# Feed-forward groups of 3, 6, 6, 7 chunks in place of 4, 6, 6, 6, with two block splits moved into the first seven-product step

## What is computed

```python
def swiglu(h, w_gate, w_up, w_down):
    return (jax.nn.silu(h @ w_gate) * (h @ w_up)) @ w_down

x = x + 0.5 * swiglu(rms_norm(x, norm_g[layer, 0]), ffn_w_gate[layer, 0], ffn_w_up[layer, 0], ffn_w_down[layer, 0])
```

## Time and profile before

| | us |
|---|---|
| median of 3 runs | 1987.91 (1987.78 to 1988.09) |
| profiled execution | 1988.24 |
| its span, first to last instruction | 1986.4 |
| PE busy | 1978.6 (13462 matmuls) |
| DVE busy | 1418.2 |
| ACT busy | 932.5 |
| POOL busy | 964.0 |
| granted clock of TensorE | 0.999 of full speed |

### The profile page before, as it was taken

How to read it: one execution, slowest core, us unless ns; L and a number is a source line. 1 busy time by engine, 2 the same in 40 slices (tenths; PEclk the granted TensorE clock), 3 DMA queues, 4 the chain that set the end, 5 groups by cost and what they waited for, 6 DMA issues and landing times. The chain is left out here.

```text
span 1986.4 us, 35197 instructions
## 1 busy us (share of the span) xinstructions
PE 1978.6 (100%) x13462; PEld 1957.5 (99%) x13462; DVE 1418.2 (71%) x2263; ACT 932.5 (47%) x1642; POOL 964.0 (49%) x1043
## 2 busy tenths in 40 slices
PE   9999999999999999999999999999999999999998
PEld 8999999999999999999999999999999999999998
DVE  5778687664766667878766668778767866878665
ACT  6354454543434435445455345454545535455443
POOL 2556666632000055676663336666743355666643
PEclk9999999999999999999999999999999999999999
DMA  6232324323222223232432222323332223232412
GB/s 162 74 86 70 101 70 117 101 58 95 66 64 65 56 73 86 77 95 69 117 102 75 64 65 75 96 80 91 102 109 70 67 57 86 77 99 65 122 38 86
DMA packets 312853, 165.28 MB, mean 83 GB/s; under 512 B 15539, under 2 KB 310271, under 8 KB 312688
## 3 DMA queue, kind: packets, MB, share of 16 engines
q1 hardware_dynamic: 307840, 157.31, 28.4%
q0 software_dynamic: 2672, 4.65, 1.0%
q10 hardware_dynamic: 2176, 1.07, 0.2%
HBM read 159.01 MB, written 4.00 MB: 82 GB/s over the span
## 5 line engine op out<-in xcount | busy, mean ns | idle before, releaser
L2401 POOL TENSOR_TENSOR sums<-in_raw,sums 128x256 f32<-128x256 f32 (+1 forms) x416 | 440.1, 1088 | 12.1 <-DVE in_lo L1751 3.9
L2401 POOL TENSOR_TENSOR sums<-in_raw 128x256 f32<-128x256 f32 (+1 forms) x208 | 179.9, 885 | 429.7 <-DVE in_lo L1751 377.4
L895 PE MATMUL psum<-xg_hi,in_lo 128*128 128x320 f32 x1152 | 356.0, 309 | 0.0
L893 PE MATMUL psum<-xg_hi,in_hi 128*128 128x320 f32 x1152 | 355.9, 309 | 0.0
L894 PE MATMUL psum<-xg_lo,in_hi 128*128 128x320 f32 x1152 | 355.9, 309 | 0.0
L1751 DVE TENSOR_TENSOR in_lo<-in_raw,in_hi 128x1024 fp32r<-128x1024 f32 (+1 forms) x208 | 271.9, 1309 | 42.5 <-ACT in_hi L1306 42.2
L893 PE MATMUL psum<-mix_hi,in_hi 128*128 128x320 f32 x864 | 267.0, 309 | 0.0
L894 PE MATMUL psum<-mix_lo,in_hi 128*128 128x320 f32 x864 | 267.0, 309 | 0.0
L895 PE MATMUL psum<-mix_hi,in_lo 128*128 128x320 f32 x864 | 267.0, 309 | 0.0
L1306 ACT ACTIVATE in_hi<-in_raw 128x1024 fp32r<-128x1024 f32 (+1 forms) x208 | 205.0, 991 | 111.7 <-PE psum L895 111.7
L744 PE MATMUL psum<-xg_hi,in_hi 128*128 128x320 f32 x800 | 252.3, 315 | 0.9 <-DVE in_lo L1792 0.6
(11 more groups left out here) (267 smaller groups left out, 4560.9 us busy)
## 6 DMA issues: line engine op xcount, KB each, us to landing
in_raw<-in_ffn_w_gate SPq DMA_DIRECT2D x87, 512.0 KB, 5.2
in_raw<-in_ffn_w_up SPq DMA_DIRECT2D x86, 512.0 KB, 4.0
in_raw<-in_ffn_w_down SPq DMA_DIRECT2D x64, 384.0 KB, 4.0
out_raw<-in_ffn_w_down SPq DMA_DIRECT2D x32, 384.0 KB, 3.5
out_raw<-in_ffn_w_down SPq DMA_DIRECT2D x32, 256.0 KB, 2.9
in_raw<-in_mix_w_in SPq DMA_DIRECT2D x14, 512.0 KB, 4.6
out<-y_nat SPq DMA_DIRECT2D x5, 512.0 KB, 3.1
in_raw<-in_mix_w_in SPq DMA_DIRECT2D x8, 256.0 KB, 4.5
```

The lines of the kernel that those rows point to most:

```text
L893: pe.matmul(dst, w_hi[:, k], v_hi, start=k == 0 and slot in (0, 1, 4), stop=False, skip_group_check=True)
L895: end = pe.matmul(dst, w_lo[:, k], v_hi, start=False, stop=k == wide - 1, skip_group_check=True)
L2401: last = pool.tensor_tensor(to[:, part], a[:, part], b[:, part], op)
```

## The change

The groups become 3, 6, 6, 7: one chunk of each feed-forward is no longer classical at the input but has a seven-product step in group 3. The numbers of units and splits are now derived from `PLAIN`; the six input units are listed in `PLAIN_UNITS`. Group 3 gets a seventh hidden slot (`last_hi`, `last_lo`, over the weight sums) and wider tiles for its output weights; its upper half is kept in `pair_even`, and so the sum of squares is cleared only behind the group's last hidden split. The output banks of group 3 move by one, as its last step has the other parity.

The block splits get a new order. T3 is split behind the sixth and now last input unit; B11 and B21 at (0, 1) of the output units; T2 at (1, 1), on DVE behind a wait for T4's source; T1 at (1, 3). B22 and T4 go into the first seven-product step: B22 ahead of its first copy, T4 behind the splits of the second step's first weights. The weights of the first step stay at (2, 3), (3, 1) and (3, 3).

The core of the diff:

```diff
-GROUPS = (4, 6, 6, 6)
+GROUPS = (3, 6, 6, 7)
+PLAIN_UNITS = [(0, 0), (1, 0), (0, 1), (1, 1), (2, 0), (2, 1)]
+LAST_K = GROUPS[3]
...
+        last_hi = over("last_hi", [P, TOKENS], arena + 30720, F32R)
+        last_lo = over("last_lo", [P, TOKENS], arena + 33280, F32R)
+        last_out_hi = over("last_out_hi", [P, 2, LAST_K, P], OUT_HI, F32R)
+        last_out_lo = over("last_out_lo", [P, 2, LAST_K, P], OUT_LO, F32R)
...
+            return 4 + (q + (g == 3)) % out_banks(g, i)
...
-        BLOCKS = ["T3", "T2", "B11", "B21", "T1", "T4", "B22"]
+        BLOCKS = ["T3", "B11", "B21", "T2", "T1", "B22", "T4"]
...
 def before_k(k):
     if g == 0 and i == 0 and j == 0 and k == 0:
-        pe.wait_ge(hidden_lo, 44 * index + 2 * gk - (2 if half == 0 else 0))
+        pe.wait_ge(hidden_lo, 44 * index + 2 * gk - (1 if half == 0 else 0))
...
 # ACT, in_step
+                if s % N_STEPS == 0:
+                    block_split("B22")
                 copy(s, fast, 0)
...
+                if s % N_STEPS == 0:
+                    act.wait_ge(block_made, 8 * index + MADE["T4"])
+                    act.wait_ge(block_lo, 7 * index + BLOCKS.index("T1") + 1)
+                    block_split("T4")
...
 # DVE, in_step
+                if s % N_STEPS == 0:
+                    block_split(index, "B22")
                 if behind:
                     gate_high(s - 1, fast - 1)
...
+                if s % N_STEPS == 0:
+                    block_split(index, "T4")
                 if behind:
                     lower_split(index, g, i - 1)
...
 # DVE, ffn (ACT has the matching lines)
+                    if q == 5:
+                        block_split(index, "T3")
 
                 def blocks_between(i, q):
-                    if (i, q) == (0, 3):
+                    if (i, q) == (0, 1):
                         block_split(index, "B11")
                         block_split(index, "B21")
                     elif (i, q) == (1, 1):
-                        block_split(index, "T1")
+                        dve.wait_ge(block_made, 8 * index + MADE["T4"])
+                        block_split(index, "T2")
                     elif (i, q) == (1, 3):
-                        block_split(index, "T4")
-                    elif (i, q) == (2, 1):
-                        block_split(index, "B22")
+                        block_split(index, "T1")
                     elif (i, q) == (2, 3):
...
+                        dve.wait_ge(hidden_lo, hidden_at(index, g, gk - 1, 1))
+                        for half in range(2):
+                            dve.memset(ss[:, half], 0.0).then_inc(ss_cleared, 1)
```

More of the change, by code:

```diff
@@ L27 @@
 SEVEN = (1, 2)
-assert sum(GROUPS) == FT and max(GROUPS) == SLOTS
+assert sum(GROUPS) == FT and len(PLAIN_UNITS) == 2 * PLAIN
 CHUNK, WINDOW, HD = 64, 128, 64
@@ L137, in weight_slot, with ends @@
     return 7 if slot == 5 and s % N_STEPS % 2 else slot
+def ends(fast):
+    return fast % FAST in (5, 11, 18)
 def read_at(fast, which):
-    order = ("low gate", "high up", "high gate") if fast % 6 == 5 else ("low gate", "high gate", "high up")
+    order = ("low gate", "high up", "high gate") if ends(fast) else ("low gate", "high gate", "high up")
     return 3 * fast + order.index(which) + 1
 def copy_at(fast, slot):
-    return 3 * fast + ((0, 2, 4) if fast % 6 == 5 else (0, 4, 2)).index(slot) + 1
+    return 3 * fast + ((0, 2, 4) if ends(fast) else (0, 4, 2)).index(slot) + 1
 def hidden_at(index, g, i, half):
@@ L876, in out_unit @@
                     before_k(k)
[L877 to L878 removed]
+                    last = product(psum[:, 4 + v % banks if bank is None else bank, 0:HALF], weights[0][:, d % 2, k], weights[1][:, d % 2, k],
+                                   moving[0](k), moving[1](k), k == 0, k == group_k - 1)
                 last.then_inc(out_mm, 1)
@@ new lines, in ffn @@
+                for q, (f, half) in enumerate(PLAIN_UNITS):
+                    b = q % 2
+                    u = 44 * index + q
+                    plain = 2 * PLAIN * index + q
+                    unit = IN_UNIT[phase] + q
+                    bank = in_bank(phase, q)
+                    if q in (0, 2) and index:
+                        norm_factor(m, half)
+                    if q == 2 and not index:
+                        start_factor(1)
+                    dve.wait_ge(in_mm, unit + 1)
+                    wait(dve, hidden_done, u - 1)
+                    dve.tensor_tensor(t1[:, b], psum[:, bank, 0:HALF], rstd[:, half], ALU.mult).then_inc(gate_scaled, 1)
+                    wait(dve, hidden_lo, u - 1)
+                    dve.tensor_tensor(f_t2[b], psum[:, bank + 1, 0:HALF], rstd[:, half], ALU.mult).then_inc(in_read, 1)
+                    if q == 0 and not index:
+                        start_factors(1)
+                    dve.wait_ge(silu_done, plain + 1)
+                    dve.wait_ge(in_read, unit + 1)
+                    dve.tensor_tensor(f_t2[b], f_t2[b], t1[:, b], ALU.mult).then_inc(hidden_done, 1)
+                    hidden_split(f, half, u + 1, f_t2[b])
+                    if index == 0 and q == 3:
+                        out_lo_split(f_out_hi, f_out_lo, 0, 0, GROUPS[0])
+                        out_lo_split(f_out_hi, f_out_lo, 1, 1, GROUPS[0])
+                    if q == 2 and index:
+                        in_lo_split((IN_CHUNK[phase] + q) % 2, SPLIT_CHUNK[phase] + q)
+                    if q == 0 and index > 0:
+                        dve.wait_ge(kv_stored, 16 * 4)
+                        dve.wait_ge(conv_stored, 16 * 2)
+                    if index == 0 and q == 1:
+                        in_lo_split((q + 1) % 2, q + 1)
+                    if q < 4:
+                        normalised(index, m, *((b11_f, "B11", 0, 0), (b21_f, "B21", 1, 0), (b12_f, "B12", 0, 1), (b22_f, "B22", 1, 1))[q])
+                    if q == 5:
+                        block_split(index, "T3")
```

163 lines of the change are left out of this document (61 added, 102 removed).

## The result

The changed kernel takes **2011.49 us** (median; 2010.18 to 2013.03) against 1987.99 us, a ratio of 1.0119 (95% interval 1.0101 to 1.0136): 1.2% slower. The forecast was 2001.9 us, its high end 2010.7. The direction was right, the size was not, and the time lies just outside the range. The profiled execution took 2010.95 us.

A forecast was written before the change was run, and what follows sets the result against it. TensorE was taken as the bound: 1988.24 - 7.06 (fewer matmuls) + 4 x 5.2 (pauses) + 1.0 (ffn0) - 0.8 (group 3) = 2002.2, the median 0.33 lower at 2001.9 us. Range 1996.9 to 2010.7 us.

The forecast's parts named there:

- high end: Whole kernel: 4 x 6.9 us of pauses plus 2 in ffn0 and no gain in group 3, 2010.7 us.
- The 48 matmuls: TensorE, four feed-forwards: 12 fewer matmuls each at 0.147 us, -7.06 us, all on the bound.
- The pauses: Group 0's output units: TensorE waits for late lower halves, 5.2 us per feed-forward, plus 1.0 in ffn0.
- The third unit: Group 0's third output unit: TensorE waits about 0.75 us for the lower hidden half.
- The extra in ffn0: ffn0's group 0: T2's lower half waits until GpSimd has made T4, +1 us (0 to 2).
- near misses: Group 0 after the fifth unit: chunks 4, 5, 6 ready about when wanted; taken as nothing, 0.6 us at the top.
- The clock: TensorE behind the pauses: the sum took no fall; rival: half clock costs 5 us more per feed-forward, 2022 us, chance 0.12.
- a sign of being wrong: Profile after: prediction wrong if no such output-weight wait appears, it stands at another unit, or the granted clock falls.
- GpSimd's hold-up: Group 0's output units: GpSimd's work slows VectorE's B11 and B21 splits, 0.54 us added once per feed-forward.
- B22 and T4 in the first step: First seven-product step: VectorE has room for both splits, cost nothing; 0.5 us per feed-forward if the cover were gone.
- Group 3: Group 3's output: last hidden chunk wanted 0.44 us later, removing a 0.2 us wait in each feed-forward, -0.8 us.
- work decides: Rival, group 0's output units: VectorE's total work counts, not its order; 2.4 us late each, 1989.6 us, chance 0.07.

The follow-up runs named there:

- experiment 2: Changed kernel with B11 and B21 split at (0, 3), behind the lower halves of output chunks 2 and 3, as in the kernel before: 2000.75 us.
- experiment 5: Changed kernel with GpSimd's four block differences replaced by zeros in ffn1 to ffn3: 2010.08 us.
- experiment 4: Kernel before with only the splits of B22 and T4 put in the first seven-product step: 1987.96 us, ratio 0.9999.
- experiment 8: Splits moved into the first step, T3, T4 and four ScalarE high parts earlier: 1998.04 us with groups 3, 6, 6, 7; 2000.48 us with 4, 6, 6, 6.
- spread: Changed kernel with T3 behind the fifth input unit (ffn0: eighth output unit), B11, B21 apart, T1 later, T2 at the first step's start: 1998.18 us.
- late_splits_2: Changed kernel with T2, T3 and weight parts 2 to 4 in the first step, T4 at its end, four ScalarE high parts earlier: 1998.04 us.
- order_alone: Kernel before (groups 4, 6, 6, 6) with only B11 and B21 moved forward from (0, 3) to (0, 1) of the output units: 2003.38 us.
- two_splits_in_step: Kernel before with only the splits of B22 and T4 put in the first seven-product step: 1987.96 us.
- late_splits_3: late_splits_2 with T4's low part moved behind the second step's first gate operation, ahead of the operation on the up sums: 1985.77 us, ratio 0.9990.

## Why the prediction was right in direction and short in size

**The 48 matmuls (-7.06).** Right: 13414 against 13462, and each stretch has the length of its count.

**The pauses (4 x 5.2 + 1.0 = 21.8).** Right in place, cause and nearly in size: 23.1 us. The fifth unit starts 10.52 us after the group's start in ffn1; the sum had 10.5 (9.95 and 0.54 for GpSimd). That this agrees to 0.03 us is partly luck: T3 started 0.27 us earlier than laid out, and the pair of splits, the weight split and the restart took as much longer. The third unit waits 0.6 us (0.75 predicted). The extra in ffn0 is 1.3 us in two later pauses (1.0 predicted). That the later units of ffn1 to ffn3 run through was right too, though for them the near misses were never tested: with the long pause gone (experiment 2) they turned into waits of 0.9 us.

**The clock (taken as nothing, with a rival at 0.12).** This is the step that failed: the sum had no term for slow matmuls behind the pauses. The clock fell in or right behind all four long pauses and cost 8.6 us by the spacing of the rows, some 7.3 us by the filled pauses: most of the 9.6 us between 2001.9 and 2011.5. The pauses were 1.3 us longer than the sum had them, group 3 gave 0.9 us more. The prediction had named the fall of the clock, as a rival and as a sign of being wrong, but set the chance low; its ground was that no row of before shows the lower level. That was no evidence: before, TensorE never paused over 1.1 us, so its trace says nothing of what follows a pause of 5 us. The rival's own price was wrong the other way, 5 us for each network, against 1.7 to 2.6. It took 5 us of matmuls at double spacing, where 5 us at half the clock lose only half of that, and in ffn1 the low level began inside the pause (0.73 in the window 723 to 725), in which it costs nothing. The pattern that the prediction cites from the Trainium skill, page "TensorE: Matmul & The Clock Gate", section "HAM oscillation — how this bites in real kernels", was the one to follow: the trace agrees, with 0.50 behind each long pause of the changed kernel. The sum had only to carry it as a term. (The high end's own terms, less the 0.33 us, add up to 2010.45 and not 2010.7; the measured time lies above both.)

**GpSimd's hold-up (0.54 once).** Right in size in ffn1 and ffn3 (0.4 us of the long pause, experiment 5), too small in ffn2 (1.0 us). The rule of the Trainium skill, page "SBUF — State Buffer", section "Who interferes with whom", allowed 1.8; the pair of splits took 3.54 us in ffn1 and 4.12 in ffn2, against 2.88 with GpSimd quiet, so the traces show 0.66 and 1.24.

**B22 and T4 in the first step (nothing).** Right: 0.9999 (experiment 4). The step has room, but not for everything; experiment 8 filled it until a gate operation came late.

**Group 3 (-0.8).** Right in sign, too small: it gave 1.7 us, 0.3 in each network and 0.4 more in ffn2.

**Order or amount.** The sum saw only order, and the prediction gave the rival "work decides" 0.07. As a forecast of the time the rival failed (1989.6). As a mechanism it holds in part. With the order undone VectorE is busy 24.1 us in a group for which TensorE needs 21.2: there the amount, GpSimd's hold-ups included, is more than fits. From `spread` on it is busy 18.8 to 20.0 us, which fits, and still 3.25 and 2.1 us are lost; late_splits_2 loses only 0.8 with no less work (19.2), by what experiment 8 made earlier. So moving work out was needed, but it was not enough, and which of the edits of 8 closed the rest was not shown. The prediction had the number at hand: VectorE's 24.2 us in the group of before (waits included), less 3.3, is 20.9 us for a stage of 21.2 us, full, with no room for GpSimd's hold-ups or for any wait.

## What to carry to other kernels

When a change shortens a stage of the engine that is the bound, add up the in-order work of the next engine in that stage before looking at its order: if it fills the shorter stage, reordering alone moves the waits (here 4.4 us a network stayed lost), and work has to go to a stage with room, each piece behind what is wanted sooner. Where it fits, single pieces that come late still cost (3.25 us with VectorE 20.0 of 24.4 us busy). Where a sum gives pauses of several us on TensorE, put the slow matmuls behind each pause into it as a term. That the trace of before shows no such fall says nothing if it has no such pause.

## What was not expected of the hardware

- The granted clock fell in or behind all long pauses of the changed kernel (4.55 to 5.13 us), three of 4.17 us and one of 3.43 us, but not behind three of 2.94 to 2.96 us in order_alone. Yet in late_splits_2 it fell behind three of four pauses of 2.0 us. In ffn2 the pause has the same place and the same 2.03 us as in ffn1, and the window behind it reads 1.00:

```profile
1177.00:1179.00 2.00, 2.00 (x15) 2.00 (x15) 1.10 (x3) 2.00 (x5) 1.31 (x2) 1.00 0.61 173
```

  So the length of the pause alone doesn't decide it. It doesn't even take a long one: in two_splits_in_step the clock reads 0.50 from 1522 to 1524, behind ffn2, and in the 12 us ahead of that TensorE is never idle for more than 0.3 us; the same place in the kernel before reads 1.00. What decides it was not settled.
- An unused matmul in the pause is worth its instruction: thirty of them, some 4.6 us, kept the clock at 1.00 and saved 5.8 us over four networks, though the unit behind them started 0.6 us later in two of the four.
- A weight split of 128x384 took 0.54 us with GpSimd at rest and up to 1.30 us beside its sums, and a wide split 1.49 or 2.03 us. In a stage that is full these steps of half a microsecond are what remains in the end: the last 0.7 us in each network of late_splits_3 is one such split at 1.17 us.
